# Splitting weights late, moving a norm, giving bias and values their own order in a hybrid attention and expert kernel

## The reference, cut to what matters

```
proj   = rms_norm(x) @ w_in                     # q, k, v of two mixers, and gates
o_diff = (softmax(q1 k1 + b) - lam * softmax(q2 k2 + b)) @ v     # 4 heads
y_diff = rms_norm(o_diff) * (1 - lambda_init)
y_na   = softmax(q k + b_na, window only) @ v                    # 8 heads
x     += (g_diff * (y_diff @ w_br_diff) + g_na * (y_na @ w_br_na)) @ w_out
x     += expert_choice_ffn(rms_norm(x))         # 16 experts, top_k of tokens each
```

## Time and profile before

| | |
|---|---|
| median of 3 runs | 2247.36 us (2246.98 to 2247.92) |
| the profiled execution, its own time | 2247.78 us |
| its span in the profile | 2246.0 us |
| PE busy in the span | 2154.8 us (96%) |
| DVE, ACT, POOL busy | 1586.4, 1373.0, 180.5 us |
| mean DMA rate | 278 GB/s |

### The profile page before, as it was taken

How to read it: one execution, slowest core, us unless ns; L and a number is a source line. 1 busy time by engine, 2 the same in 40 slices (tenths; PEclk the granted TensorE clock), 3 DMA queues, 4 the chain that set the end, 5 groups by cost and what they waited for, 6 DMA issues and landing times.

```text
span 2246.0 us, 30582 instructions
## 1 busy us (share of the span) xinstructions
PE 2154.8 (96%) x11924; PEld 1873.9 (83%) x11924; DVE 1586.4 (71%) x1264; ACT 1373.0 (61%) x1118; POOL 180.5 (8%) x140
## 2 busy tenths in 40 slices
PE   6989979999995999999999999999999999999997
PEld 5857868888775898999988899898998989999896
DVE  5375334223447888888888888888888888888885
ACT  4364335222224677776777767677776777777774
POOL 1202200000013000010100101010010100101000
PEclk9999979999996999999999999999999999999999
DMA  5110142112415999999999999999999999999994
GB/s 228 57 56 25 57 134 70 62 57 113 162 67 205 362 380 353 386 365 370 375 368 372 367 378 374 367 377 365 378 366 375 369 358 391 359 373 372 366 382 173
DMA packets 71582, 623.99 MB, mean 278 GB/s; under 512 B 8336, under 2 KB 8720, under 8 KB 18800
## 3 DMA queue, kind: packets, MB, share of 16 engines
q1 hardware_dynamic: 63264, 595.62, 68.7%
q0 software_dynamic: 7840, 27.40, 4.3%
q10 hardware_dynamic: 432, 0.34, 0.0%
HBM read 609.70 MB, written 13.63 MB: 278 GB/s over the span
## 4 chain that ended last, share of the span: by engine, by line
PE 86%; DVE 5%; ACT 3%; issue 3%; DMA 2%; POOL 0%; ACTq 0%; DVEq 0%; POOLq 0%
PE PS L492 26%; PE PS L494 26%; PE PS L493 26%; DVE x_w_low L1114 2%; ACT x_w_high L1047 2%; PE PS L589 2%; PE PS L574 1%; PE PS L833 1%; PE PS L602 1%; PE PS L501 1%; DVE hidden L1465 1%; DMA bias_windows<-in_bias_prompt 1%; DVE s L1221 0%; ACT w_high L852 0%; PE PS L700 0%
## 5 line engine op out<-in xcount | busy, mean ns | idle before, releaser
L1114 DVE TENSOR_TENSOR x_w_low<-x_w_raw,x_w_high 128x2816 fp32r<-128x2816 f32 (+1 forms) x382 | 1176.6, 3090 | 244.0 <-ACT x_w_high L1047 242.4
L1047 ACT ACTIVATE x_w_high<-x_w_raw 128x2816 fp32r<-128x2816 f32 (+2 forms) x384 | 978.7, 2557 | 251.8 <-PE PS L494 212.0
L492 PE MATMUL PS<-x_w_high,xT_high 128*96 128x352 f32 x2048 | 667.9, 326 | 1.4 <-DVE xT_low L1114 1.4
L494 PE MATMUL PS<-x_w_high,xT_low 128*96 128x352 f32 x2048 | 660.7, 323 | 0.0
L493 PE MATMUL PS<-x_w_low,xT_high 128*96 128x352 f32 x2048 | 658.3, 321 | 0.0
L492 PEld LDWEIGHTS PS<-x_w_high,xT_high 128*96 128x96 f32 x2048 | 330.7, 161 | 6.8 <-issue 4.4
L493 PEld LDWEIGHTS PS<-x_w_low,xT_high 128*96 128x96 f32 x2048 | 332.9, 163 | 2.4
L494 PEld LDWEIGHTS PS<-x_w_high,xT_low 128*96 128x96 f32 x2048 | 332.3, 162 | 1.4
L492 PE MATMUL PS<-x_w_high,hidden_high 128*96 128x512 f32 x704 | 280.3, 398 | 2.2 <-DVE x_w_low L1114 1.1
L493 PE MATMUL PS<-x_w_low,hidden_high 128*96 128x512 f32 x704 | 278.4, 395 | 0.0
L494 PE MATMUL PS<-x_w_high,hidden_low 128*96 128x512 f32 x704 | 278.0, 395 | 0.0
(11 more groups left out here) (182 smaller groups left out, 1745.8 us busy)
## 6 DMA issues: line engine op xcount, KB each, us to landing
x_w_raw<-in_w_expert_gate SPq DMA_DIRECT2D x128, 1408.0 KB, 8.3
x_w_raw<-in_w_expert_up SPq DMA_DIRECT2D x128, 1408.0 KB, 8.8
x_w_raw<-in_w_expert_down SPq DMA_DIRECT2D x96, 1536.0 KB, 8.4
x_w_raw<-in_w_expert_down SPq DMA_DIRECT2D x32, 1024.0 KB, 6.9
w_raw<-in_w_in SPq DMA_DIRECT2D x20, 1024.0 KB, 4.8
x<-in_x_sample SPq DMA_DIRECT2D x8, 512.0 KB, 13.6
bias_windows<-in_bias_sample POOLq DMA_DIRECT2D x8, 512.0 KB, 3.7
w_raw<-in_w_out SPq DMA_DIRECT2D x4, 1024.0 KB, 4.8
```

The source lines that it names most:

```text
L492: mm(out, sh, mh, start=first, stop=False)
L494: return mm(out, sl, mh, start=False, stop=last)
L1047: a_(xh[:, w % SPLITS, 0:n], xraw[:, w % RAWS, 0:n], ACT.Copy).then_inc(x_high, 1)
L1114: return v.tensor_tensor(out, src, high.bitcast(F32), ALU.subtract)
```

## The change

The change touches seven places.

1. The second unit of the next stage is split in the tail of `attend` (step `len(L) + 1`) and no longer at the end of the v chunk.
2. The norm of `yd` moves into the v chunk of `project("pn")`: ACT squares its tiles there, and DVE norms one after each value tile (`norm_y`).
3. The v chunk of "pn" takes the sample tiles first (`V_ORDER`). Stores and windows count on semaphores by row half and by window pair, and PE waits for each pair by itself; `v_windows0` and `v_windows1` change places in memory.
4. The eight prompt tables of "na" come in four loads of two heads into four buffers of their own, two after the last bias of "diff" and two after its last output. The sample tables keep two buffers.
5. SP waits until ACT has made the high part of the last `w_out` unit before it starts the expert weights.
6. `ranks` compares with a column of zeros in a `tensor_tensor` where it had a `tensor_scalar`.
7. POOL signals when its first gather is issued, and DVE starts the one-hot tables of the other experts only then; PE turns the first expert's tokens between the second and the third of their products.

```diff
+V_ORDER = {"pd": [0, 1, 2, 3, 4, 5], "pn": [2, 3, 4, 5, 0, 1]}
...
-              for i, off in enumerate((38848, 42944))]
+              for i, off in enumerate((42944, 38848))]
+        bias_p = [at(f"bias_prompt{i}", off, 2 * PW) for i, off in enumerate((44992, 46016, 47040, 48320))]
...
+        def second_unit(br):
+            return [c[2] for c in CHUNKS if c[0] == {"diff": "pn", "na": "g"}[br]][0] + 1
... SP
-                    for t in range(2, NT):
-                        sp.wait_ge(S("pn", "pused"), 2 * NT + t + 1)
-                        sp.dma_start(v_dram[(t - 2) * P:(t - 1) * P, :], vv[:, t, :]).then_inc(s_vst, 16)
-                    sp.wait_ge(s_vst, 64)
-                    for j, c0 in enumerate(WINDOWS):
-                        for half in range(2):
+                    for half in range(2):
+                        for t in range(2 + 2 * half, 4 + 2 * half):
+                            sp.wait_ge(S("pn", "pused"), 2 * NT + V_ORDER["pn"].index(t) + 1)
+                            sp.dma_start(v_dram[(t - 2) * P:(t - 1) * P, :], vv[:, t, :]
+                                         ).then_inc(s_vst[half], 16)
+                    for half, j in ((0, 0), (0, 1), (1, 0), (1, 1), (0, 2), (0, 3), (1, 2), (1, 3)):
+                        sp.wait_ge(s_vst[max(half, j // 2)], 32)
...
             sp.wait_ge(S("o", "m_t"), 2 * NT)
+            sp.wait_ge(w_high, UNITS)
             with sp.Fori(0, E) as e:
... POOL
+            def load_diff(h):
+                if h >= 2:
+                    pool.wait_ge(S("diff", "biased"), NT * (h - 1))
+                pool.dma_start(bias[:, h % 2, :], bias_diff[h]).then_inc(s_b[h % 2], 16)
+            def load_prompt(i):
+                pool.dma_start(bias_p[i], bias_prompt[i]).then_inc(S("na", f"bias_prompt{i}"), 16)
+            def load_sample(h):
+                pool.wait_ge(S("na", "biased"), 4 * (h % 2) + 4 if h < 2 else 16 + 4 * (h - 1))
+                pool.dma_start(bias_w[:, h % 2, :], bias_sample[h]).then_inc(S("na", f"bias_sample{h % 2}"), 16)
...
-            for nh in range(2, 6):
-                load_bias(nh)
+            load_diff(2)
+            load_diff(3)
+            pool.wait_ge(S("diff", "biased"), len(ATT["diff"]))
+            load_prompt(0)
+            load_prompt(1)
+            pool.wait_ge(S("diff", "out"), len(ATT["diff"]))
+            load_prompt(2)
+            load_prompt(3)
+            norm_rs("pn", 12, 8)
             norm_rs("yd", NT, 4)
-            norm_rs("pn", 12, 8)
-            for nh in range(6, len(BIAS)):
-                load_bias(nh)
+            for h in range(8):
+                load_sample(h)
...
             gather(0)
+            nc.gpsimd.memset(small[:, 310:311], 0.0).then_inc(S("rt", "gather_issued"), 1)
... PE
-                        if windowed and h == 0 and qt == 0:
-                            pe.wait_ge(s_vw, 16 * 8)
+                        if windowed and h == 0 and qt % 2 == 0:
+                            pe.wait_ge(s_vw[qt // 2], 16 * 4)
...
+            table_products(0)
+            table_products(1)
             pe.wait_ge(S("rt", "tables"), 1)
             pe.wait_ge(S("x", "xe"), 16)
             for q in range(PRE):
                 transpose_tokens(q)
+            table_products(2)
+            table_products(3)
... ACT, project
-                    split_units(u0 + nu + 2)
+                    if kind == "v" and stage == "pn":
+                        act.wait_ge(S("pn", "ss"), 2 * NT)
+                        for t in range(NT):
+                            square("yd", t, y_tok["diff"][:, t, :])
+                    if kind != "v":
+                        split_units(u0 + nu + 2)
... ACT and DVE, attend
                 for step in range(len(L) + 5):
+                    if step == len(L) + 1:
+                        split_units(second_unit(br) + 1)
... ACT, between attend("diff") and project("pn")
-            for t in range(NT):
-                square("yd", t, y_tok["diff"][:, t, :])
-            act.wait_ge(S("yd", "ss"), NT)
... DVE, project
+            def norm_y(t):
+                reduce_sq("yd", t, 4, 128)
+                if t > 0:
+                    y = y_tok["diff"][:, t - 1, :]
+                    scale_q("yd", t - 1, y, y, 4, 128)
+                if t == NT - 1:
+                    y = y_tok["diff"][:, t, :]
+                    scale_q("yd", t, y, y, 4, 128)
...
-                            v.tensor_scalar(vv[:, t, :], PS[:, t, :], nrs[:, t:t + 1], None, ALU.mult
+                            v.tensor_scalar(vv[:, tile, :], PS[:, t, :], nrs[:, tile:tile + 1], None, ALU.mult
                                             ).then_inc(S(stage, "pused"), 1)
+                            if stage == "pn":
+                                norm_y(t)
...
-                link(v.tensor_scalar(sel, out, 0.0, None, ALU.is_lt))
+                link(v.tensor_tensor(sel, out, zero.to_broadcast((E, w)), ALU.is_lt))
...
+            dve.wait_ge(S("rt", "gather_issued"), 1)
             for t in range(4):
                 one_hot(G[:, t], rk[:, t, :], CS).then_inc(S("rt", "G"), 1)
```

More of the change, by code:

```diff
@@ L229, in encoder @@
         one = small[0:E, 168:169]
+        zero = small[0:E, 169:170]
         aff = small[:, 200:296].rearrange("p (t e) -> p t e", t=NT)
@@ L241, in encoder @@
         s_b = [sem(f"bias_loaded{b}") for b in range(2)]
-        s_vst = sem("values_stored")
-        s_vw = sem("value_windows_loaded")
+        s_vst = [sem(f"values_stored{half}") for half in range(2)]
+        s_vw = [sem(f"value_windows_loaded{i}") for i in range(2)]
         s_pha = sem("act_done_with_stage")
@@ L273, in encoder, with bias_of @@
                "na": [(h, qt, t0, 2) for (t0, nt) in GROUPS for h in range(8) for qt in range(nt)]}
[L277 to L283, removed]
+        def bias_of(br, h, t0, qt):
+            if br == "diff":
+                return bias[:, h % 2, 384 - 128 * qt:]
+            if t0 == 0:
+                return bias_p[h // 2][:, PW * (h % 2) + 128 - 128 * qt:]
+            return bias_w[:, h % 2, NW * qt:]
         def window_order(a):
@@ L511, in chunk_product @@
                 n = u0 + u
+                tile = V_ORDER[stage][t] if kind == "v" else t
                 if t == 0:
@@ L768, in _, with table_products @@
             i.then_inc(S("rt", "first_slots"), 1)
-            for t in range(4):
+            def table_products(t):
                 pe.wait_ge(S("rt", "G"), t + 1)
@@ L1212, in attend @@
                         n = nt * P
-                        nh = h if br == "diff" else 4 + h if t0 == 0 else 12 + h
-                        if qt == 0 and (br == "na" or t0 == 0):
-                            dve.wait_ge(s_b[nh % 2], 16 * (nh // 2 + 1))
+                        if qt == 0 and t0 == 0:
+                            dve.wait_ge(*((s_b[h % 2], 16 * (h // 2 + 1)) if br == "diff" else
+                                          (S("na", f"bias_prompt{h // 2}"), 16)))
+                        elif qt == 0 and br == "na":
+                            dve.wait_ge(S("na", f"bias_sample{h % 2}"), 16 * (h // 2 + 1))
                         dve.wait_ge(S(br, "log"), a + 1)
@@ L1218, in attend @@
                             dve.wait_ge(S(br, "tr"), a - 3)
-                        c0 = {"diff": 384 - 128 * qt, "na": 128 - 128 * qt if t0 == 0 else NW * qt}[br]
+                        table = bias_of(br, h, t0, qt)[:, 0:n]
                         for m in range(nm):
@@ L1252, in _ @@
             attend("diff")
-            for t in range(NT + 1):
-                if t < NT:
-                    reduce_sq("yd", t, 4, 128)
-                if t > 0:
-                    y = y_tok["diff"][:, t - 1, :]
-                    scale_q("yd", t - 1, y, y, 4, 128)
             project("pn")
@@ L1315, in _ @@
             v.memset(one, 1.0)
+            v.memset(zero, 0.0)
             dve.wait_ge(S("rt", "g2"), 16)
@@ L1529, in _prompt_bias @@
             out[:, GW * rr + c, :, kc] = rpb[:, 5 - rr:11 - rr, kc - c + 15].transpose(2, 0, 1)
-    return out.reshape(8, P, PW)
+    return out.reshape(4, 2, P, PW).transpose(0, 2, 1, 3).reshape(4, P, 2 * PW)
 def _sample_bias(rpb):
```

26 lines of the change are left out of this document (12 added, 14 removed).

## The result

The changed kernel takes 2217.03 us (median of 4 runs, 2215.21 to 2218.18) against 2247.17 for the kernel before in the same comparison: a ratio of 0.9864, 95% interval 0.9849 to 0.988, 30 us or 1.4% faster. 2217.0 was forecast. The profiled execution took 2217.34, its span is 2215.5, that of before 2246.0: 30.5 us apart, to be found between landmarks of the two traces. The four runs of the changed kernel lie 3 us apart, so a hit to a tenth is luck.

The account below looks back on a forecast made before the run. PE, busy 96% of the span, bounds the kernel; only its waits and low-clock time can be won. Terms 4.3 + 4.7 + 16.8 + 2.5 + 1.6 + 0.6 = 30.5 us off 2247.8 give 2217.3 us; range 2210 to 2230.

Parts of the forecast that it names:

- Starts of "diff" and "pn": Attention half: moving the split wins 4.3 us in "diff"; moving the `yd` norm wins 4.7 us in "pn".
- Prompt heads: Start of "na": early table loads end the bias waits; one more slow PE step, then full clock; 16.8 us won.
- Rival (b): PE stays at the low clock through the prompt heads of "na": 14.5 us of gain lost, 2231.8 us; chance 0.11.
- Who could be late next: Window copies and sample tables in "na": copies issued by 309, needed at 321; no wait expected, but one may return here.
- Rival (c): Sample tables or windows come late in "na" because loads crowd: 3 to 4 us lost, 2221 us; chance 0.08.
- Stage "o": Last `w_out` unit: holding back expert loads cuts its transfer from 7.2 to 5.5 us; 2.5 us won, bounds 0 and 4.1.
- Ranks: Comparison opening the sample tokens' ranks: as `tensor_tensor` it takes 0.69 us without waiting for POOL; 1.6 us won.
- rival (a): In the ranks, the new comparison waits for POOL's subtraction after all: 2219.3 us; chance 0.25.
- First gather: Before the first expert: held up by DVE's one-hots; issued alone, it brings the first product 0.6 us sooner.
- Rival (d): The first gather, before the experts, is slow by itself: 2221.5 us; chance 0.06.
- Rival (e): Expert loop takes longer per expert, PE and weight streaming both near their end: 2254 us at 2.3 us more each; chance 0.03.

Follow-up runs that it names:

- part 4 alone: Kernel before, with only the prompt tables in four own buffers, loaded during and right after "diff": 2241.32 us against 2246.18, ratio 0.9979.
- the version with the norm's tail moved: Changed kernel, with the last reduce and last two scales of the `yd` norm moved among the first ten maps of "na": 2218.04 us, ratio to before 0.9876.

## Why the prediction was right, and where its terms were off

**Starts of "diff" and "pn".** Right in mechanism and size: 4.26 for 4.3, 4.88 for 4.7. Undoing part 1 put the same 7.16 us back. That PE keeps its clock behind the short stop in "diff" held in nine of eleven executions; in the other two it fell, for 1.9 and 0.5 us.

**Prompt heads.** The waits for tables went as forecast, and most of the gain is there, 18.8 for 16.8. But the step gave it to part 4 alone, which by itself won 4 of it. The term took more steps at the low clock than the changed kernel has: from first bias to first sample values it and its variants took 20.2 to 21.2 us, where the step gave 22.4; part 4 alone, with a longer stop and low clock, had 22.3. Rival (b) is out: where the clock fell at the start of "na", and no tables were waited for, it was at 1.00 again 3 to 5 us after PE's restart.

**Who could be late next.** This is the step that was weakest. It counted the copies as there when issued, "issued by 309", 12 us ahead of their use. They land later: in part 4 alone PE had them 15.9 us after the last issue, in the version with the norm's tail moved 13.4 after (issue ended at 297.7). From these and the last issue at 296.70 they land at 310.1 to 312.6 in the changed kernel, by estimate, and its second pair is asked for at 312.1: two microseconds to spare at best. Rival (c) came in small: DVE waits 1.91 for the third head's table, and the sample heads take 1.14 longer. One reason why the copies are slow is seen in the windows at the start of "na": while nothing else moves, the DMA share is 0.26 and the rate 99 to 102 GB/s, at which eight copies of 256 KB (2.1 MB) need 21 us. The Trainium skill, page "DMA: Bandwidth & Descriptors", section "Why a DMA increments its semaphore by 16 and not by 1", says that a transfer uses the largest number of engines, up to 16, that divides the outermost dimension of both its patterns; a copy here reads 4 rows of the grid and writes 128 partitions, so 4 engines of 16. The share of 0.26 agrees. A copy with 16 in front was not tried. The other reason that the traces offer is the traffic behind them, the weight loads and tables of the run with part 4 alone.

**Stage "o".** The step failed in its cause: it blamed the expert loads, and without part 5 the transfer was no slower (5.8 us, one run). The experiments show the gain's load on POOL's queue, which the prediction did not look at. Held back, it gives the 4.8 us transfer. The size, 0.64 measured in the profiled pair for 2.5 taken, says little: over the eight executions with part 5 it is 0.1 to 2.2, with the clock at the restart, and none of it is shown to be part 5's.

**Ranks.** The 1.6 failed, and rival (a) happened, chance 0.25: -0.26. The nearest row taken was one beside a small POOL operation. The rule in the Trainium skill, page "SBUF — State Buffer", section "Who interferes with whom", said that a DVE instruction with two SBUF inputs contends with a GpSimd instruction that reads SBUF. The trace agrees, 2.60 us with both in SBUF beside 0.68 with one in PSUM. The old comparison, with one tensor in SBUF and a constant, waited as well (2.33 to 2.35 us); that is not explained by two inputs, and no run here tests it.

**First gather.** Right, and larger: 1.16 for 0.6, 1.14 when undone. Rival (d) is out.

**Expert loop.** The 2.1 us after the first product are scatter: over the 14 profiled executions, before and part 4 alone among them, that stretch took 1540.7 to 1542.8, and part 4 alone, with the old code there, 1540.9. Rival (e) is out.

So that 2217.0 was hit so closely is luck: it came out through two terms too large (ranks and stage "o", together 3.7 us), one wait not priced (1.14), and against these fewer slow steps at "na" (2.0, of which 0.9 is the clock of that execution, which the wait takes back), the gather (0.6) and scatter (2.1).

## What to carry to other kernels

When a wait is removed, follow the next loads to their landing, not to their issue: here a removal that was to win 16 us won 4 by itself, because the copies behind it landed late. Where an operation of one engine waits for another engine to finish, look at where its operands lie: one operand in PSUM won what a change of operation did not. Before two transfers on one queue are parted, look at what the other queues issue in the same microseconds. Before a stretch is priced from one execution, look at the same kernel's second: the clock behind a stop alone moved stretches here by 1 to 2 us.

## What the runs showed of the hardware that was not expected

A DVE operation that reads one operand from PSUM ran beside POOL's 12.24 us subtraction at its own length (0.68) and did not stretch it. An indirect gather takes POOL 1.02 us with DVE's one-hots held until it is issued and 4.43 beside them (two SBUF inputs each), ending 0.9 after them. The same 3.4 us stop of PE, in the same program, left the clock at 1.00 in one execution and at 0.62 from 289 to 293 us in another. Eight copies on one queue take 14.86 us to issue, four 2.8. A load of 1 MB took 6.5 to 7.0 us with one of 512 KB issued 1.2 us ahead of it on another queue, 4.8 without.
